# A two-layer and one-block model on one core: stick-breaking attention's sums over keys in high and low parts, and its last gates emptied in two groups

## The reference, cut to what matters

```
def stick_breaking(q, k, v):            # scale = Dh ** -0.5, query blocks of 128
    z = einsum('bthd,bshd->bhts', q[:, q0:q1], k[:, :q1]) * scale
    strict = key index < query index
    log_beta = log_sigmoid(z)
    log_1m = where(strict, log_sigmoid(-z), 0)
    after = cumsum(log_1m, axis=3, reverse=True) - log_1m
    w = where(strict, exp(log_beta + after), 0)
    out = einsum('bhts,bshd->bthd', w, v[:, :q1])

y = concatenate([yc, yd], axis=-1) * silu(gate)      # yc of gla, yd of stick_breaking
x = x + gate_res * (y @ out_w)
```

## Time and profile before

| | |
|---|---|
| median of 3 runs | 960.37 us (960.01 to 960.43) |
| the profiled execution's own time | 960.04 us |
| its span, first to last instruction | 958.3 us |
| TensorE busy | 935.9 us, 98% |
| DVE busy | 643.6 us, 67% |
| ACT busy | 522.8 us, 55% |
| DMA | 172.30 MB, mean 180 GB/s |

### The profile page before, as it was taken

The page is one execution under the profiler, slowest core; times in us unless marked ns, Lnnn a source line. Parts: engine busy times, 40 slices in busy tenths (PEclk is TensorE's granted clock), DMA queues, the critical chain, the costliest instruction groups (busy, mean ns, idle before and its releaser), DMA issues.

```text
span 958.3 us, 19474 instructions
## 1 busy us (share of the span) xinstructions
PE 935.9 (98%) x8621; PEld 907.2 (95%) x8621; DVE 643.6 (67%) x741; ACT 522.8 (55%) x614; POOL 2.1 (0%) x14
## 2 busy tenths in 40 slices
PE   7899999999999999999999999999999999999998
PEld 7899999999999999899899999999889999999998
DVE  2897887865677456566689876555676665466565
ACT  3445454445554467963476663467656654454445
POOL 0000000000000000000000000000000000000000
PEclk9999999999999999999999999999999999999999
DMA  9999557874566443367445443243326467556521
GB/s 340 362 366 325 174 176 237 287 227 149 160 221 222 144 153 115 115 204 241 133 139 172 133 134 111 68 132 133 99 72 215 133 206 230 180 176 197 178 89 44
DMA packets 153439, 172.30 MB, mean 180 GB/s; under 512 B 4000, under 2 KB 137692, under 8 KB 153228
## 3 DMA queue, kind: packets, MB, share of 16 engines
q1 hardware_dynamic: 151696, 167.43, 54.3%
q10 hardware_dynamic: 1660, 3.63, 1.1%
HBM read 170.00 MB, written 1.05 MB: 178 GB/s over the span
## 4 chain that ended last, share of the span: by engine, by line
PE 49%; DVE 5%; ACT 3%; issue 1%; POOL 0%; POOLq 0%; DVEq 0%
PE pj L2593 39%; PE pj L2552 1%; PE m_all L2043 1%; PE pj L2553 1%; ACT w_hi L930 1%; PE pj L2554 1%; PE m_all L2316 1%; PE m_all L2299 1%; PE m_all L2443 1%; PE pj L2409 1%; DVE w_lo L1432 0%; DVE work L1860 0%; PE m_all L2302 0%; PE m_all L2470 0%; DVE small L1861 0%
## 5 line engine op out<-in xcount | busy, mean ns | idle before, releaser
L1432 DVE TENSOR_TENSOR w_lo<-raw,w_hi 128x2048 fp32r<-128x2048 f32 (+1 forms) x126 | 285.5, 2269 | 134.7 <-ACT w_hi L930 134.1
L2593 PE MATMUL pj<-h_hi,w_hi 128*128 128x256 f32 x1224 | 347.2, 284 | 2.9 <-DVE h_lo L1869 1.1
L2593 PE MATMUL pj<-h_lo,w_hi 128*128 128x256 f32 x1224 | 341.6, 279 | 0.0
L2593 PE MATMUL pj<-h_hi,w_lo 128*128 128x256 f32 x1224 | 341.5, 279 | 0.0
L930 ACT ACTIVATE w_hi<-raw 128x2048 fp32r<-128x2048 f32 (+1 forms) x126 | 237.9, 1890 | 54.2 <-PE pj L2593 28.6
L2593 PEld LDWEIGHTS pj<-h_hi,w_hi 128*128 128x128 f32 x1224 | 228.9, 187 | 8.1 <-issue 5.8
L2593 PEld LDWEIGHTS pj<-h_lo,w_hi 128*128 128x128 f32 x1224 | 229.0, 187 | 0.3
L2593 PEld LDWEIGHTS pj<-h_hi,w_lo 128*128 128x128 f32 x1224 | 228.9, 187 | 0.2
L2593 PE MATMUL pj<-y_hi,w_hi 128*128 128x256 f32 x592 | 166.0, 280 | 1.1 <-issue 0.9
L2593 PE MATMUL pj<-y_hi,w_lo 128*128 128x256 f32 x592 | 165.4, 279 | 0.0
L2593 PE MATMUL pj<-y_lo,w_hi 128*128 128x256 f32 x592 | 165.1, 279 | 0.0
(11 more groups left out here) (399 smaller groups left out, 1122.5 us busy)
## 6 DMA issues: line engine op xcount, KB each, us to landing
raw<-in_odd_in_w_dram SPq DMA_DIRECT2D x28, 1024.0 KB, 5.3
raw<-in_w_in_dram SPq DMA_DIRECT2D x23, 1024.0 KB, 5.4
raw<-in_ada_w_dram SPq DMA_DIRECT2D x22, 1024.0 KB, 7.3
raw<-in_w_ff_in_dram SPq DMA_DIRECT2D x16, 1024.0 KB, 5.4
raw<-in_w_ff_out_dram SPq DMA_DIRECT2D x16, 1024.0 KB, 5.5
raw<-in_even_in_w_dram SPq DMA_DIRECT2D x13, 1024.0 KB, 5.8
raw<-in_even_out_w_dram SPq DMA_DIRECT2D x8, 1024.0 KB, 5.9
raw<-in_odd_out_w_dram SPq DMA_DIRECT2D x8, 1024.0 KB, 5.4
```

Source lines behind the costliest of these rows:

```text
L1432: V.tensor_tensor(lo[:, 0:n], raw_of(u)[:, 0:n], hi[:, 0:n].bitcast(F32), ALU.subtract).then_inc(done, 1)
L2593: m = nc.tensor.matmul(to, a_, b_, start=(s == 0 and q == 0 and (fb == 0 or not together)), stop=(s == len(steps_) - 1 and q == 2), skip_g ...
```

## The change

**The sums.** At head 0 DVE copies the constants `from_here` and `ones` into rounded form (`sb_const`). For each head DVE, in `sb_z`, now rounds the masked softplus into `sb_hi` (a cast of 128x384) and subtracts it into `sb_lo`. `sb_c` on TensorE is four matmuls in place of two, all of the rounded kind: the triangle and the ones on `sb_hi`, then on `sb_lo`.

**The gates.** The first five gate jobs are projected in their slots but not emptied there (`early`). gga0, gga1 and gga2 are emptied behind the steps of gga2's slot, gga3 and ggb0 behind those of ggb0's slot. A table with the exponential is loaded only behind gga2's silu (`log_exp_next`). The list `gates`, which numbers them, takes in jobs that are emptied this way.

```
-    log_exp_next = [(name, i) for name in ("gga", "ggb") for i in range(4)][:len(left)]
-    for i in range(8):
-        odd("gga" if i < 4 else "ggb", "gate", 5136 if i < 4 else 6160, i % 4)
-        for st in left[i] if i < len(left) else []:
-            step(*st)
-        if i >= 4:
-            schedule.append(("ada_out", gate_units[i - 4]))
-    assert len(left) <= 8
+    log_exp_next = [("gga", 2)]
+    gate_jobs = [("gga", i) for i in range(4)] + [("ggb", i) for i in range(4)]
+    for n, (name, i) in enumerate(gate_jobs):
+        odd(name, "gate", 5136 if name == "gga" else 6160, i)
+        if n < len(left):
+            early(name, i)
+            for st in left[n]:
+                step(*st)
+        if n in (2, 4):
+            for key in gate_jobs[0:3] if n == 2 else gate_jobs[3:5]:
+                finish(*key)
+        if n >= 4:
+            schedule.append(("ada_out", gate_units[n - 4]))
+    assert len(left) == 5
...
-        gates = [k for kind, k in schedule if kind == "job" and jobs[k]["kind"] in ("gate", "relu2")]
+        gates = [k for kind, k in schedule if kind in ("job", "evacuate") and jobs[k]["kind"] in ("gate", "relu2")]
...
+        sb_const = tuple(work_r[:, 55, a:a + P] for a in (0, P))
+        sb_hi, sb_lo = (work_r[:, 52:56, :].rearrange("p c t -> p (c t)")[:, a:a + 384] for a in (0, 384))
...
             def sb_z(h):
+                if h == 0:
+                    for to, name in zip(sb_const, ("from_here", "ones")):
+                        link(V.tensor_copy(to, K(name)))
...
-                V.tensor_tensor(sbw(2), sbw(2), K("sb_mask"), ALU.mult).then_inc(S("sb_l"), 1)
+                link(V.tensor_tensor(sbw(2), sbw(2), K("sb_mask"), ALU.mult))
+                link(V.tensor_copy(sb_hi, sbw(2)))
+                V.tensor_tensor(sb_lo, sbw(2), sb_hi.bitcast(F32), ALU.subtract).then_inc(S("sb_l"), 1)
...
-                nc.tensor.matmul(M[1][:, 0:384], K("from_here"), sbw(2), start=True, stop=False, skip_group_check=True)
-                nc.tensor.matmul(M[1][:, P:2 * P], K("ones"), sbw(2)[:, 2 * P:3 * P], start=False, stop=True, skip_group_check=True).then_inc(S("sb_c_done"), 1)
+                from_here, ones = sb_const
+                for part in (sb_hi, sb_lo):
+                    nc.tensor.matmul(M[1][:, 0:384], from_here, part, start=(part is sb_hi), stop=False, skip_group_check=True)
+                    m = nc.tensor.matmul(M[1][:, P:2 * P], ones, part[:, 2 * P:3 * P], start=False, stop=(part is sb_lo), skip_group_check=True)
+                m.then_inc(S("sb_c_done"), 1)
```

## The result

| | before | changed |
|---|---|---|
| median | 960.37 us (958.91 to 961.19) | 963.27 us (963.12 to 965.65) |
| the profiled execution, its span | 960.04, 958.3 | 963.12, 961.3 |
| first z product (head 0) to first v product of head 7 | 69.62 | 71.61 |
| first z product to first matmul of the output projection | 88.79 | 93.19 |
| from there to the end of the span | 536.44 | 536.09 |

Both medians are of five runs. The ratio is 1.0037, 95% interval 1.0022 to 1.0052: the changed kernel is 0.2 to 0.5% slower. In the last four experiments' session, on chip 13, it was 1.0048 [1.0035, 1.0062] (run changed_again).

The account below looks back on a forecast made before the run. TensorE, busy 98% of the span, was taken as the bound, with DVE's longer round making it wait. A later last v product, 2.3, plus a clock fall, 1.2, gave 3.5 us on 960.04; forecast 963.9 us, range 961.7 to 966.2.

Parts of the forecast that it names:

- `sb_c` on TensorE: Sums in each head's slot: forecast to fall from 0.87 to 0.55 us, 0.32 us a head less for TensorE.
- DVE's round: DVE's closed cycle per head: forecast 7.90 us, longer than TensorE's new 7.46, so TensorE waits 0.45 before each `sb_c`.
- the rival of the slow cast: DVE's new cast takes 0.56 instead of 0.36 us, 1.6 more over eight rounds: 965.5 us; chance 0.13.
- The chain to the last head: DVE's rounds followed from head 0, then the gates, to head 7's v product: `sb_o` forecast at 405.0, before at 402.69.
- The term of 2.3: Forecast delay, in us, of the v product of head 7 (`sb_o`) and all jobs behind it.
- the rival with the shorter last wait: TensorE's wait before `sb_o` of head 7 is shorter by 1 us or more, no clock fall: 961.5 us; chance 0.14.
- The clock: TensorE's 5.3 us wait before head 7's v product likely drops its clock to 0.50: forecast cost 1.2 us.
- The sum: Whole kernel: 2.3 for the later v product plus 1.2 for the clock, 3.5 us slower.
- Nothing gives it back later: Behind `sb_o` of head 7 no later wait absorbs the delay; jobs through the output projection all move by 2.3 us.
- The clock holds: Rival: TensorE's clock does not fall at the wait before head 7's v product, only 2.3 remains: 962.7 us; chance 0.16.
- DVE's round under TensorE's: Rival: DVE's round under 7.46 us, TensorE sets the pace, `sb_o` of head 7 1.8 earlier: 958.6 us; chance 0.09.

Follow-up runs that it names:

- changed_again: The changed kernel itself run once more, on chip 13, against the kernel before: 964.13 us, ratio 1.0048.
- e7: The changed kernel with the cast of the masked softplus done twice: 966.79 us, ratio to the kernel before 1.0078.
- e4: The changed kernel with DVE's masked z moved ahead of its wait for ACT's logarithm: 959.35 us, ratio to the kernel before 0.9997.
- e3: The changed kernel with eleven unused 32-bit matmuls put before the v product of head 7: 961.55 us, ratio to the kernel before 1.002.
- e2: The kernel before with only the changed gate schedule, sums still with 32-bit operands: 960.67 us, ratio 1.0013.
- e1: The kernel before with only the sums in high and low parts, gates emptied in their slots as before: 961.86 us, ratio 1.003.
- e5: The kernel before, 32-bit sums, with gates emptied in groups of one, one and three and the next unit's split ahead of the first two: 957.27 us, ratio 0.9976.
- e6: Sums in high and low parts, masked z ahead of the logarithm wait, gates grouped one, one, three with split ahead: 955.78 us, ratio to the kernel before 0.9963.

## Why the prediction was right

It gave 963.9 (961.7 to 966.2) and the median is 963.27. The place, the releaser and the sign of each step held; one term, the clock's, was given half of what it measured, and the agreement of the total owes something to chance. By steps:

- **`sb_c` on TensorE**, 0.55 forecast, 0.60 measured. The two matmuls of 128 columns are cheap, 0.06 each by starts. By the Trainium skill, "TensorE: Matmul & The Clock Gate", "Back-to-back issue gap", 128 columns by themselves take 0.056 at the full clock, and the rows agree, although each of these has a weight load. The same section has 0.081 for a stream of such matmuls with weight loads, which no row here shows. For 384 columns an estimate by its formula is 0.163, and there the rows differ: 0.26 and 0.22. I had put 0.35 for the two of 384 columns, which took 0.48, and some 0.20 for the two of 128, which took 0.12; so I was 0.05 short. It changed nothing, as forecast: TensorE does 0.27 us a head less, and from head 4 on waits 0.36 before each `sb_c`.
- **DVE's round**, 7.90 forecast, 7.87 measured. The cast is 0.36 (median of eight 0.360), so the rival of the slow cast is out. The 0.36 came from the slope of one kind of instruction and the fixed part of another, a copy from PSUM; the nearest row, L1864 at 384 elements, takes 0.42, so its exactness is partly luck. e7 shows that this round sets the pace and e4 that it need not.
- **The chain to the last head.** Put into the time base of the changed profile (1.05 earlier), I had L1940 of head 0 at 339.78 and it came at 339.81; head 6 at 387.15, and it came at 387.00; L1940 of head 7 at 402.80, and it came at 402.47; the v product at 403.95, and it came at 403.63. The term of 2.3 is 1.99 in the trace, 0.15 less for the six rounds and 0.18 for the handing over between the gates. The wait was 5.3 forecast, 4.98 measured. That is no case of the rival with the shorter last wait, which asked for 1 us or more.
- **The clock**, 1.2 forecast. This is the step that was mis-sized. I took the low stretch at the end of the trace of before, 3.3 us (3.42 by windows of 1 us), as the length of any such stretch, let part of it fall in the wait, and came to 1.2. Here it lasted 6.84 us, twice that, 401.8 to 408.6. Some 1.8 us of it lay in the wait and 5.0 in work, and half of 5.0 is 2.5. The trace has 2.41 (8.67 us from the v product of head 7 to the next one-column matmuls, 6.26 before), and e3 has 2.30 by taking the fall away. That TensorE was still idle when the clock fell is what these runs have beside the longer stretch: the clock was low for twice as long here, in changed_again and in e7 (wait 5.0, low at the restart) as in e2 and e4 (waits of 2.64 and 3.04, falls 0.3 to 1 us behind the restart). A fall inside a wait is not needed for a long stretch, though: at the ends of e1, e3 and e5 the clock fell while TensorE was doing the sixteen transposes (at 955.9, 955.2 and 950.2), and was still low 4.8 to 5.4 us on, at the end of the span; TensorE had gone idle in between. All falls of the ten traces ahead of the last 15 us lasted 3.4 us, but for the one in each of the three traces with the wait of 5.0. What makes a stretch twice as long stays open. The fall at 951.5 in the earlier trace rows, from which I took the length, was no case of a long wait either: TensorE had one-column matmuls there, with 0.48 us idle between them.
- **The sum** was 3.5 and should have been 1.99 + 2.41 = 4.40. The first comparison of medians gave 2.9, the second 5.1; by the ratios the intervals are 2.1 to 5.0 and 3.4 to 5.9, and 4.4 lies in both. That 963.9 lies so near to 963.27 is therefore partly chance: in the profile, 1.05 us came from an earlier first z and 0.35 from a shorter rest, which are no part of my working.
- **Nothing gives it back later**: right. From the v product of head 7 to the output projection there is no further wait, and all jobs there moved by the sum.
- **The clock holds**, the rival, gave 962.7 for the changed kernel; the trace has the fall. Its ground, that 1.8 us of idleness left the clock at 1.00, was one case of an event that goes either way at such lengths (last section).
- **DVE's round under TensorE's**, the rival on the faster side, had the price nearly right and the condition wrong. It doesn't need cheaper instructions. It needs one that does not depend on ACT's last step to stand ahead of the wait. e4 did that: round 7.45, and the v product of head 7 at 68.20, 1.4 before its old place, where the rival said 1.8.

What stood in the profile of before and I didn't use: DVE's idle 2.47 us in the earlier trace rows, which I named in a rival for the two new instructions, stands two instructions ahead of L1667, which needs the scaled z and the mask and not the logarithm that DVE waits for there.

## What to carry to other kernels

Work taken from the engine that is busy 98% of the time is worth nothing if it is paid for on the path that this engine waits for: add up the closed round of each engine (which instruction hands to which, back to the first) before and after, and take the longest. Before anything is shortened, look for an instruction on that path that could stand in an idle stretch ahead of a wait; here that was worth 3.4 us, more than all that the sums gave. When deferred work is put behind a step in program order, ask what of the next critical step stands behind it in each queue: the same gates cost 2.25 us with three of them emptied ahead of the last exponential (e2), and brought 2.15 with one ahead of it, one a slot earlier and three behind (e5).

## What was not expected of the hardware

- The price of a wait of TensorE can be more than its length. In the traces of the attention, waits of 2.05 and 2.10 (e1), 2.64 (e2), 3.04 (e4) and 4.98 us (changed kernel) were each followed by, or held, a fall to 0.50; those of 0.50 (e1) and 1.23 (before) were not. It cost 1.7 us behind the waits of 2.64 and 3.04, and 2.3 to 2.4 behind that of 4.98.
- But the length of a wait does not settle whether the clock falls. In the first 30 us of the program, where TensorE waits for DMA, idle stretches of 2.02 us (e1, up to 9.58) and 1.75 us (e6, up to 24.80) were followed by a fall within 1 us, and one of 2.62 us (e2) was not:

```profile
25.98 0.44 PE L2049 MATMUL pj<-cst,rows 128*128 128x128 f32 x2 [2.62 <-DMA rows<-in_ple_post_norm_dram]
```

  The clock stays at 1.00 from 22 to 32 there. Around 700 us all ten traces have two waits of 0.8 and 0.96 us within 3 us; three of them (e3, e5, changed_again) have a fall behind the second, seven have none. So the same wait can cost its own length in one execution and the price of a fall on top in the next, and a single trace is not enough to price it. What decides between the two stays open.
- Matmuls without use kept the clock: 4.91 us of them in the wait saved 2.30 us behind it (e3). They mend a wait only in part, and not the wait itself.
- A wait before a matmul can be absent from both the idle column and the list of waits: 0.36 us by starts shows nowhere (changed kernel), 0.68 shows as 0.43 (e7).
